# Moving rotated rows by transfers, and a re-ordered opening, in a two-block transformer kernel

## The reference

```python
u = rms_norm(h, g_mix[l]) @ w_in[l]
qa = u[..., 0:512].reshape(B, S, 4, 2, 64)      # differential units: 4, two heads of 64 each
ka = u[..., 512:1024].reshape(B, S, 4, 2, 64)
...
def apply_partial_rope(x, cos, sin):            # ROT_DIM 16 of 64: the rest passes unchanged
    x1, x2, xp = x[..., :8], x[..., 8:16], x[..., 16:]
    return jnp.concatenate([x1 * c - x2 * s, x2 * c + x1 * s, xp], axis=-1)
...
s = einsum('bhcqd,bhckd->bhcqk', qblk, kh) * scale      # causal, Q_BLOCK = 128
p = softmax(where(mask, s, -inf))
w = p[:, :, 0] - lam * p[:, :, 1]
o = rms_norm(einsum('bhqk,bhkv->bhqv', w, vh), g_subln) * (1 - lam_init)
```

## Time and profile before

| | |
|---|---|
| median of 3 runs | 2294.36 us |
| the three runs | 2294.76, 2291.03, 2294.36 us |
| the profiled execution | 2291.01 us, its span 2289.2 us |
| PE busy | 2214.7 us, 97% of the span |
| DVE, ACT, POOL busy | 1377.4, 952.1, 700.9 us |
| first scores of unit 0 | at 72.58 us |
| the four differential units | from 72.58 to about 320 us |

### The profile page before, as it was taken

The page is one execution under the profiler, slowest core; times in us unless marked ns, Lnnn a source line. Parts: engine busy times, 40 slices in busy tenths (PEclk is TensorE's granted clock), DMA queues, the critical chain, the costliest instruction groups (busy, mean ns, idle before and its releaser), DMA issues.

```text
span 2289.2 us, 36425 instructions
## 1 busy us (share of the span) xinstructions
PE 2214.7 (97%) x14780; PEld 1752.0 (77%) x14780; DVE 1377.4 (60%) x1775; ACT 952.1 (42%) x1688; POOL 700.9 (31%) x436
## 2 busy tenths in 40 slices
PE   7999999998999999999999999999999999999997
PEld 4777776665788888788888888888676777778885
DVE  6777857778676544584574575323508376567554
ACT  4444457777544232354234334233416412363321
POOL 2312212121211213274564565322231133122231
PEclk9999999999999999999999999999999999999998
DMA  3211101113131001111111110112220011100022
GB/s 134 74 56 56 47 19 56 56 47 129 50 138 54 29 27 39 45 47 56 56 55 44 57 64 29 54 55 92 77 73 19 19 38 38 40 20 13 4 111 83
DMA packets 38555, 125.80 MB, mean 55 GB/s; under 512 B 3856, under 2 KB 4368, under 8 KB 37776
## 3 DMA queue, kind: packets, MB, share of 16 engines
q1 hardware_dynamic: 33936, 103.30, 13.3%
q10 hardware_dynamic: 4480, 20.49, 2.3%
HBM read 114.34 MB, written 8.91 MB: 54 GB/s over the span
## 4 chain that ended last, share of the span: by engine, by line
PE 86%; DVE 6%; ACT 4%; issue 3%; POOL 1%; DMA 0%; ACTq 0%; DVEq 0%; POOLq 0%
PE PS L184 23%; PE PS L186 22%; PE PS L185 22%; PE PS L2305 2%; PE PS L776 2%; PE PS L753 1%; PE PS L1212 1%; PE PS L938 1%; PE PS L903 1%; PE PS L920 1%; DVE arena L1024 1%; PE PS L312 1%; PE PS L1915 1%; PE PS L1775 1%; PE PS L1788 1%
## 5 line engine op out<-in xcount | busy, mean ns | idle before, releaser
L233 POOL TENSOR_TENSOR w_hi<-w_raw,const 128x1024 fp32r<-128x1024 f32 x77 | 152.0, 1974 | 1096.6 <-PE PS L184 985.9
L184 PE MATMUL PS<-u_r,w_hi 128*128 128x512 f32 x1184 | 477.6, 403 | 9.0 <-DVE h L590 3.1
L186 PE MATMUL PS<-u_r,w_lo 128*128 128x512 f32 x1184 | 462.1, 390 | 0.0
L194 POOL TENSOR_TENSOR w_lo<-w_raw,w_hi 128x1024 fp32r<-128x1024 f32 (+1 forms) x143 | 330.7, 2313 | 323.2 <-ACT w_hi L190 308.3
L185 PE MATMUL PS<-arena_r,w_hi 128*128 128x512 f32 (+1 forms) x888 | 331.9, 374 | 0.0
L184 PEld LDWEIGHTS PS<-u_r,w_hi 128*128 128x128 f32 x1184 | 222.5, 188 | 62.0 <-DVE h_r L194 6.5
L186 PEld LDWEIGHTS PS<-u_r,w_lo 128*128 128x128 f32 x1184 | 222.4, 188 | 47.7
L184 PE MATMUL PS<-h_r,w_hi 128*128 128x512 f32 x512 | 207.8, 406 | 1.8 <-POOL w_lo L194 1.5
L186 PE MATMUL PS<-h_r,w_lo 128*128 128x512 f32 x512 | 200.2, 391 | 0.0
L185 PE MATMUL PS<-y_r,w_hi 128*128 128x512 f32 x512 | 199.5, 390 | 0.0
L1556 DVE TENSOR_TENSOR h<-h,PS 128x512 f32<-128x512 f32 x288 | 181.6, 683 | 21.6 <-PE PS L186 17.6
(11 more groups left out here) (434 smaller groups left out, 4280.4 us busy)
## 6 DMA issues: line engine op xcount, KB each, us to landing
w_raw<-in_w SPq DMA_DIRECT2D x174, 512.0 KB, 3.4
arena<-in_w SPq DMA_DIRECT2D x10, 512.0 KB, 5.0
h<-in_xT ACTq DMA_DIRECT2D x1, 4096.0 KB, 14.4
u<-parked_stream ACTq DMA_DIRECT2D x1, 4096.0 KB, 12.8
out<-arena SPq DMA_DIRECT2D x16, 256.0 KB, 2.0
parked_stream<-h ACTq DMA_DIRECT2D x6, 512.0 KB, 2.6
h<-in_xT SPq DMA_DIRECT2D x8, 256.0 KB, 6.7
h<-in_xT ACTq DMA_DIRECT2D x8, 256.0 KB, 8.8
```

The source lines that it names most:

```text
L184: first = pe.matmul(out, a[0], b[0], start=start, stop=False)
L186: return first, pe.matmul(out, a[1], b[0], start=False, stop=stop)
L194: return e.tensor_tensor(out, x, hi_part.bitcast(F), ALU.subtract)
L233: pool.tensor_tensor(out, src, cst("ones")[:, 0:1].broadcast_to([P, D]), ALU.mult).then_inc(S("w_high"), 1)
```

## The change

1. The constant matrix `rot` and the chunks "r" are gone. When q or k of a unit has been copied out of PSUM (its second half), ACT issues four transfers of 8 rows x 1024, which copy rows 8 to 15 to rows 0 to 7 and the reverse, for both heads, into `heads(w)`. The sign has moved into the angles' frequencies. The other rows of `heads` are set to zero once, by four memsets on DVE. `rope_dve` waits for all eight transfers of a unit.
2. The filler of a unit's rows is dealt anew: rows 4 to 7 get a half chunk of v each. Before, row 4 had two "r", row 5 two "r" and a whole chunk of v, rows 6 and 7 a half chunk of v.
3. The opening: q and k of unit 0 are made together, piece by piece in turns (`first_pair_pe`). All eight squares of the first half are summed on PE. Those of the second half are added on DVE in two groups of four, with two sums on PE before the seventh piece. The positions are loaded before the second half of x, and six of the eight steps of the angles stand ahead of the first scaling on DVE. The second panel is loaded to a place of its own (`early_raw`) and POOL splits it with no wait for PE; the large constants move from ACT's queue to SP's.

```diff
-                  ("ident", 128), ("rot", 128), ("masks", 192), ("blk64", 128),
+                  ("ident", 128), ("masks", 192), ("blk64", 128),
...
-            f[b + m] = np.float32(500000.0) ** np.float32(-(2.0 * (m % 8)) / 16.0)
+            f[b + m] = np.float32(500000.0) ** np.float32(-(2.0 * (m % 8)) / 16.0) * (1 if m >= 8 else -1)
...
         def split_unit_panel(pool, m):
-            if m > 0:
+            if m == 1:
+                pool.wait_ge(S("panel_mem_in"), 16)
+                pool.sem_inc(w_in[0], 16)
+                pool.tensor_tensor(w_hi[:, 1, :], early_raw, cst("ones")[:, 0:1].broadcast_to([P, D]), ALU.mult).then_inc(S("w_high"), 1)
+                pool.wait_ge(S("w_high"), 2)
+                low(pool, w_lo[:, 1, :], early_raw, w_hi[:, 1, :]).then_inc(S("w_split"), 1)
+                return
+            if m > 1:
                 pool.wait_ge(S("weight_free"), m + CREDIT)
...
-        FIRST_CHUNKS = [("q", 0, 0), ("k", 0, 0), ("q", 0, 1), ("r", 0, 0), ("r", 0, 1), ("k", 0, 1), ("r", 0, 2), ("r", 0, 3),
-                        ("v", 0, 0), ("v", 0, 1), ("t", 0, 0), ("t", 0, 1)]
+        FIRST_CHUNKS = [("q", 0, 0), ("k", 0, 0), ("q", 0, 1), ("k", 0, 1), ("v", 0, 0), ("v", 0, 1), ("t", 0, 0), ("t", 0, 1)]
         def da_parts(i, s):
             w = i + 1
-            if s >= 6:
-                return ([(("ada", i, 0), None)] if s == 7 else []) + [(("v", w, 1), s - 6)] + ([(("t", w, 0), None)] if s == 7 else [])
-            o = [[("o", i - 1, h)] if i > 0 else [] for h in range(2)]
-            r = [[("r", w, n)] if w < N_DA else [] for n in range(4)]
-            whole = {0: ([("t", i, 1)] if i > 0 else []) + [("q", w, 0)], 1: [("q", w, 1)], 2: [("k", w, 0)] + o[0], 3: [("k", w, 1)] + o[1],
-                     4: r[0] + r[1], 5: r[2] + [("v", w, 0)] + r[3]}[s]
-            return [(c, None) for c in whole]
+            if s >= 4:
+                half = [(("v", w, s // 2 - 2), s % 2)]
+                return [(("ada", i, 0), None)] + half + [(("t", w, 0), None)] if s == 7 else half
+            o = [(("o", i - 1, s - 2), None)] if i > 0 and s >= 2 else []
+            t = [(("t", i, 1), None)] if i > 0 and s == 0 else []
+            return t + [(("qk"[s // 2], w, s % 2), None)] + o
...
+        def first_pair_pe(pe, h):
+            if h == 0:
+                order = [(0, 0), (1, 0), (0, 1), (1, 1)] + [(k, x) for k in range(2, KC) for x in range(2)]
+            else:
+                order = [(k, x) for k in range(KC // 2) for x in range(2)] + [(k, x) for x in range(2) for k in range(KC // 2, KC)]
+            for k, x in order:
+                if k == 0 and h == 0:
+                    panel_in(pe, x)
+                elif k == 0:
+                    pe.wait_ge(*chunk_done(("qk"[x], 0, 0)))
+                if (h, k, x) == (0, KC - 2, 0):
+                    mix_sum_pe(pe, 1, [0, MIX_ADDED])
+                if x == 0:
+                    wait_split(pe, "mix", h)(k)
+                f, m = product(pe, bank(x), W(x, k), u_mix(k, h * HALF, (h + 1) * HALF), k == 0, k == KC - 1)
+                if (h, k, x) in ((0, 0, 0), (1, KC // 2, 1)):
+                    f.then_inc(S("weight_free"), 1)
...
+            if what in "qk" and h == 1 and w < N_DA:
+                act.wait_ge(*chunk_done(c))
+                for at in (0, 64):
+                    for lo, hi in ((0, 8), (8, 0)):
+                        act.dma_start(heads(w)[x][at + lo:at + lo + 8, :], raw_qk[x][at + hi:at + hi + 8, :]).then_inc(S("rotated_in"), 16)
...
-            dve.wait_ge(*chunk_done(("r", w, 2 * x + 1)))
+            if x == 0:
+                dve.wait_ge(S("rotated_in"), 128 * (w + 1))
...
             load_main(0)
+            sync.dma_start(pos_i[:, :], pos_d).then_inc(S("pos_in"), 16)
             for k in range(4):
                 sync.dma_start(hT[:, k, HALF:T], xT_d[:, k, HALF:T]).then_inc(S("x_late"), 16)
-            load_main(1)
-            sync.dma_start(pos_i[:, :], pos_d).then_inc(S("pos_in"), 16)
-            load_main(2)
+            sync.dma_start(early_raw, w_d[2, :, :]).then_inc(S("panel_mem_in"), 16)
+            sync.dma_start(const[:, CONST_EARLY:], const_d[:, CONST_EARLY:]).then_inc(S("const_late"), 16)
+            sync.wait_ge(S("w_split"), 1 + CREDIT)
+            load_panel(4, 0)
...
+            split_dve(dve, "mix", 0, in_(hT), in_u, in_h, mix, ks=range(4))
+            for k in range(1, MIX_ADDED):
+                mix_add(dve, k)
+            split_dve(dve, "mix", 0, in_(hT), in_u, in_h, mix, ks=range(4, 7))
+            for k in range(MIX_ADDED + 1, KC):
+                mix_add(dve, k)
+            split_dve(dve, "mix", 0, in_(hT), in_u, in_h, mix, ks=range(7, KC + 1))
+            split_dve(dve, "mix", 1, in_(hT), in_u, in_h, mix)
```

More of the change, by code:

```diff
@@ L272, in summed_late @@
             return n in ("mlp", "fin", "post") and h == 1 and k % KC >= KC - 2
-        MIX_SUM = 3
-        NORM_ADDS = {n: [(k, 0) for k in range(MIX_SUM + 1, KC)] if n == "mix" else [(k, h) for k, h in NORM_SQUARES[n] if k % KC and not summed_late(n, k, h)] for n in NORM_SQUARES}
+        NORM_ADDS = {n: [(k, 1) for k in range(KC) if k % MIX_ADDED] if n == "mix" else [(k, h) for k, h in NORM_SQUARES[n] if k % KC and not summed_late(n, k, h)] for n in NORM_SQUARES}
         NORM_ROOTS = {"mix": [0, 1], "mem": [0], "x": [0, 1], "mlp": [0, 1], "fin": [0, 1], "fin1": [0, 1], "post": [0, 1]}
@@ L330, in mix_sum_pe @@
[L330 to L334, removed]
-                else:
-                    pe.wait_ge(S("norm_added"), norm_at(NORM_ADDS, "mix", (KC - 1, 0)))
-                m = pe.matmul(PS[:, NB + c.start:NB + c.stop], cst("ones"), norm_sq["mix"](k)[:, c], start=(k == 0), stop=(k == MIX_SUM))
-            m.then_inc(S("norm_summed"), 1)
+        def mix_add(dve, k):
+            c, sq, to = norm_cols("mix", 1), norm_sq["mix"], k // MIX_ADDED * MIX_ADDED
+            dve.wait_ge(S("norm_sq_ready"), norm_at(NORM_SQUARES, "mix", (k, 1)))
+            if k > to + 1:
+                dve.wait_ge(S("norm_added"), norm_at(NORM_ADDS, "mix", (k - 1, 1)))
+            dve.tensor_tensor(sq(to)[:, c], sq(to)[:, c], sq(k)[:, c], ALU.add).then_inc(S("norm_added"), 1)
@@ new lines, in mix_sum_pe @@
+        def mix_sum_pe(pe, h, ks):
+            c = norm_cols("mix", h)
+            order = list(range(KC)) if h == 0 else [0, MIX_ADDED]
+            for k in ks:
+                if h == 1:
+                    pe.wait_ge(S("norm_added"), norm_at(NORM_ADDS, "mix", (k + MIX_ADDED - 1, 1)))
+                else:
+                    pe.wait_ge(S("norm_sq_ready"), norm_at(NORM_SQUARES, "mix", (k, h)))
+                m = pe.matmul(PS[:, NB + c.start:NB + c.stop], cst("ones"), norm_sq["mix"](k)[:, c], start=(k == order[0]), stop=(k == order[-1]))
+                if k == order[-1]:
+                    m.then_inc(S("norm_summed"), 1)
@@ L657, in chunk_pe @@
                     panel_in(pe, g)
-                ready = None
-                if w == 0 and what == "q":
-                    def ready(k):
-                        if h == 0:
-                            norm_pe_chunk(pe, "mix", 1, k)
-                        wait_split(pe, "mix", h)(k)
-                m = chunk_product(pe, g, b, u_mix, h, ready=ready, free=(h == 1) if w == 0 and what == "k" else None, part=part)
+                m = chunk_product(pe, g, b, u_mix, h, part=part)
             if part != 0:
                 m.then_inc(S("proj_mm"), 1)
+        def first_pair_pe(pe, h):
[15 more added lines that the diff above has]
+                    f.then_inc(S("weight_free"), 1)
+                if k == KC - 1:
+                    m.then_inc(S("proj_mm"), 1)
         def chunk_act(act, c):
@@ L675, in chunk_act @@
                 e = act.activation(ada[:, 3 * w:3 * w + 3], b[:, 0:3], ACT.Copy)
-            elif what == "r":
-                e = act.activation(heads(w)[h // 2][:, cols], b, ACT.Copy)
             elif what == "t":
@@ L2982, in _ @@
             dve.tensor_tensor(lamt[:, 4:5], lamt[:, 3:4], lamt[:, 2:3], ALU.subtract).then_inc(S("lam_a"), 1)
-            dve.wait_ge(S("lam_a"), 2)
+            dve.wait_ge(S("lam_a"), 4)
             dve.tensor_scalar(lamt[:, 5:6], lamt[:, 4:5], LAM_INIT, None, ALU.subtract).then_inc(S("lam_a"), 1)
-            dve.wait_ge(S("lam_a"), 3)
+            dve.wait_ge(S("lam_a"), 5)
+            for x in range(2):
+                dve.memset(heads(1)[x], 0.0)
             dve.wait_ge(S("ang_ready"), 3)
@@ L3388, in _ @@
             pe.wait_ge(S("const_in"), 16)
[L3389 removed]
+            pe.wait_ge(S("lam_a"), 3)
             pe.matmul(bank(0)[:, 0:2], cst("ones"), lamt[:, 0:2], start=True, stop=True).then_inc(S("lam_sum"), 1)
[L3391 removed]
+            mix_sum_pe(pe, 0, range(KC))
             pe.wait_ge(S("lam_exp"), 1)
[L3393 to L3394 removed]
+            for h in range(2):
+                first_pair_pe(pe, h)
+            for c in FIRST_CHUNKS[4:]:
+                if c == ("t", 0, 0):
```

55 lines of the change are left out of this document (17 added, 38 removed).

## The result

The change makes the kernel slower. Its runs had a median of 2307.3 us (four, 2303.96 to 2311.86), those of the kernel before 2293.78 us: ratio 1.0062, 95% interval 1.005 to 1.0075. Repeated later, it was 2306.5 us (five) and 1.0057 (1.0044 to 1.007). I had predicted 2290, range 2281 to 2299.

The account below looks back on a forecast made before the run. PE was taken as the bound, with DVE right behind in row 5. The opening's -4.6 us and the units' +1.5 us gave -3.1 us; from 2292.8 us it predicted 2290, range 2281 to 2299.

Parts of the forecast that it names:

- Transfers on ACT, the wait that is added: Units 0 to 2, ends of rows 1 and 3: PE waits 2.0 and 1.8 us behind four issues, 11.4 us in all.
- Rotated chunks off PE: Beside units 0 to 2: twelve chunks of 0.86 us each leave PE, 10.3 us less work.
- DVE and POOL: Rows 4 to 7: DVE about even with PE, POOL's split costing 0.4 us per unit, 1.2 in all.
- a gain of 0.8: Beside unit 3, a half chunk fills row 4 where PE waited 0.82 us: minus 0.8 us.
- rival B: Rows 5 and 6: DVE becomes the bound as POOL's passes reach the rotation; total +7.1 us, 2300; chance 0.14.
- The opening: Before unit 0's first scores: these come at 68.0 instead of 72.6 us, 4.6 us earlier; ends 8.5 and 0.
- the sign that I had named: Unit 0's first scores past 71 us would show the forecast wrong and rival C right.
- rival C: The opening gives nothing, since the first root slips with the slow clock; total +1.5 us, 2294; chance 0.12.
- Rival A: Issues on ACT are cheap: at 0.33 us each 2285, chance 0.22; at no cost 2278, chance 0.12.
- the rule named in the prediction: The skill's rule that initiating a DMA is usually small; four issues on ACT would be 0.2 us, the wait vanishing.

Follow-up runs that it names:

- e8_probe: e1_sp with groups of four extra transfers on SP at its very end; an 8-row issue took 0.62 to 0.68 us from SBUF, 0.29 to 0.33 from HBM.
- e1_sp: The changed kernel with the transfers of rotated rows issued by SP in place of ACT: 2288.64 us, ratio 0.9981 to the kernel before.
- e4_fill: The changed kernel with three dummy f32 products in PE's wait in rows 2 and 4: 2299.86 us, ratio 1.0032 to the kernel before.
- e10_again: The changed kernel itself, run once more: 2306.5 us, ratio 1.0057 to the kernel before.
- e9_release: e1_sp with PE telling POOL earlier, at the end of row 3, that the weight buffer is free: 2284.64 us, ratio 0.9963; repeated, 2282.4 us, 0.9959.
- e2_one: The changed kernel with one transfer of four issued on ACT, the others left out, output wrong: 2288.97 us, ratio 0.9983 to the kernel before.
- e12_oldopen_release: e9_release with the opening of the kernel before: 2283.72 us, ratio 0.9964 to the kernel before.
- e11_openfill: The changed kernel with two dummy f32 products in the opening's wait for the third panel: 2305.54 us, ratio 1.0056 to the kernel before.
- e6_oldopen: e1_sp with the opening of the kernel before, so only units 1 to 3 are rotated by transfers: 2288.83 us, ratio 0.9984 to the kernel before.

## Why the prediction was wrong

The trace after, by my steps. Up to unit 3's last row PE is 11.2 us later than before; I had it 3.1 us earlier. Of these 14.3 us, 7.5 lie in one step (1 and 2 below), 3.3 in the opening, 1.4 in unit 3 and some 2 in smaller terms.

1. **The step that failed: "Transfers on ACT, the wait that is added."** The mechanism of the wait was right, place and all: what queues behind the issues is the copy of the turned weights, and PE has nothing else to do. The size was not. I took 0.52 us an issue from the nearest row, with 0.61 as the upper end; it is 0.632, and 0.03 between two. Four are 2.65 us, outside my range of 1.3 to 2.4. The six waits of PE, 15.3 us in all, added 14.4 (0.42 of the two in rows 4 of units 1 and 2 was there before), not 11.4. I had two rows of transfers within SBUF, 0.52 and 0.61, and took the lower, which was the first of two in a row; in e8_probe a first issue of 32 rows took 0.51 and those that followed 0.59, and 8 rows cost a little more than 16. (At the lower end, four issues in 1.3 us, my own rows give waits of 6.6 us and not 7.0; it changes nothing.)
2. **In the same step, what the wait sets off was put at nothing, and it was the larger half.** After three of the six waits the clock fell to 0.50. PE's busy time shows it against e1_sp, where the clock stays up: 8.85 against 7.03 (unit 0, row 2), 6.98 and 7.01 against 5.64 (row 4, units 1 and 2), some 4.5 us. (Rows 2 of units 1 and 2 were 0.2 us longer too, 8.10 and 8.11 against 7.90, at a clock of 1.00; why is open.) With useless work in the waits e4_fill was 6 us faster than e10_again, whose trace has five such falls. Rows 9 held the two levels, and I used them for the opening alone.
3. **Rotated chunks off PE: right.** e9_release shows the gain without the waits: rows 4 and 5 of unit 2 keep PE busy 11.68 us, against 15.00 before, 3.3 us less; I had 3.44.
4. **DVE and POOL: undecided in the changed kernel, too low without its waits.** Row 5 came to 6.04 us as predicted, since the wait gave DVE room. Row 6 took 7.08 instead of 6.51 in units 0 to 2 (in e9_release too, so it isn't POOL's collision): 1.7 us, where my whole term was 1.2. With the wait gone (e1_sp) POOL's collision cost 1.4 us per unit more. My rival B had the mechanism, not the place: row 4's weights, not the rotation. In unit 3, where I had a gain of 0.8, that collision made it a loss of 0.6; without it, in e9_release, unit 3 gains 0.8.
5. **The opening: 1.3 us, not 4.6.** The second root came at 37.58 (I had 37.6), in part by luck: the first scaling was at 19.37, 1.0 us before my 20.4, and what followed took 1.0 us longer. The wait for the third panel was 2.45 us (2.6). What failed came behind: eight issues took 5.9 us (I had counted 2.1 on the path), one of them 1.25; v ran at a clock of 0.50 to 0.65 for 3 us; and the rotation on DVE ended at 71.2, not 67.4. By the sign that I had named, first scores past 71 us, this is rival C's place, though its cause, a late first root, did not occur.

Rival A, cheap issues, is excluded by the issue rows, and with it the rule named in the prediction. The Trainium skill, "DMA: Bandwidth & Descriptors", section "Issuing engines are not separate DMA queues", calls the sequencer's time to initiate a DMA usually small relative to the DMA; here four of them were 2.65 us on the issuing engine, and what hung on that was the whole cost (e1_sp, e2_one). It also says that issuing from several engines saves only that time; here this time, the waits behind it and the slow clock after them were 17 us. The 50 ns that the prediction took from "Anatomy of one DMA" are given there for transfers issued by GpSimd; no run here has one.

On POOL against DVE the runs came first: DVE's 0.61 and 0.89 us became 1.99 and 2.86, ending shortly behind POOL's. The Trainium skill, "SBUF — State Buffer", section "Who interferes with whom", says that where the two contend, the later one blocks fully until the first is done. This trace agrees within 0.3 us: both of DVE's instructions began inside POOL's and ended 0.36 and 0.69 us behind them, a little less than their own 0.61 and 0.89.

Open is why the late stage, after about 2050 us, gives back or takes up to 5 us: the profiled changed kernel was 11.2 us behind at the units' end, 9.5 at 2050 us and 13.0 at the last; e12_oldopen_release was 6.8 us behind e9_release at 2050 us and 2.1 at its end. A part is the clock: from 2140 to 2160 us it was 0.91 in the changed kernel and 1.00 in the kernel before, which is at most some 2 us. The rest hides what an opening is worth.

## What to carry to other kernels

Replacing TensorE work by a small transfer is worth its busy time only if no engine on the path issues it: count each issue at 0.63 us (SBUF source), all that queues behind, and put it on an engine that nobody waits for. A wait of TensorE has to be priced with what may come after it: here, where the clock fell after waits of 2.5 to 2.85 us, it cost another 1.3 to 1.8 us each in the first trace and up to 3.1 in e11_openfill's, and other work ahead of the waiting instruction removed both. And when a wait goes, look at once for the collision that it had hidden, and ask whether the event that releases it can be told earlier.

## What the runs showed of the hardware

- An issue of 8 rows within SBUF takes 0.62 to 0.68 us, on ACT as on SP; the first of these on ACT took 1.25. From HBM it took 0.29 to 0.33 us on SP at the kernel's end (e8_probe), 128 rows 0.35 to 0.43 there.
- A wait of 2.5 us is followed by a low clock in one execution and not in the next (row 2 of unit 1: 10.58 and 12.18 us); so is one of 2.06 us in row 4 of unit 0 (7.69 us in the first trace, 9.28 in e10_again's). In e1_sp a wait of 2.42 us in the opening was followed by 1.00.
- Shorter waits are no safe ground: in e6_oldopen the clock was 0.80 from 73 to 76 us and 0.63 to 79, after a wait of 1.17 us before the first scores, with PE busy 2.18 us of the three before; the kernel before had one of 1.24 us at the same place and stayed at 1.00.
